# V is transposed in bulk beside the last two projection tiles; keys are transposed where V's chunk transposes stood

## The reference, cut to what matters

```python
h = rms_norm(x, p['g_pre']) * (1.0 + scale) + shift
z = h @ p['w_in']                       # 1024 -> 4096 columns
...
zc = centred_shift(zc, p['mu'])         # p + mu * (0.5 * (prev + next) - p)
r, k, v, lw, la = jnp.split(zc, [...], -1)
...
kk = kk * lax.rsqrt(jnp.sum(kk * kk, -1, keepdims=True) + 1e-12)
...
def step(s, inp):                       # per token, per head, s is value x key
    r_t, w_t, k_t, v_t, kk_t, a_t = inp
    sa = jnp.einsum('bhvk,bhk->bhv', s, kk_t)
    s = (s * w_t[:, :, None, :] - sa[..., None] * (kk_t * a_t)[:, :, None, :]
         + v_t[..., None] * k_t[:, :, None, :])
    return s, jnp.einsum('bhvk,bhk->bhv', s, r_t)
...
out = jnp.concatenate([ya, yb, yc], -1) @ p['w_out']
x = x + gate * rms_norm(out, p['g_post'])
```

## Time and profile before

| | us |
|---|---|
| median of 3 runs | 1085.96 (1084.84 to 1086.45) |
| the profiled execution | 1087.09 |
| its span, first to last instruction | 1085.3 |
| PE busy | 1005.1 (93%) |
| PEld busy | 907.3 (84%) |
| DVE busy | 641.6 (59%) |
| ACT busy | 426.4 (39%) |
| POOL busy | 409.3 (38%) |
| granted TensorE clock, mean | 0.972 of full |

### The profile page before, as it was taken

One profiled execution on the slowest core, in us unless ns is written; L12 is line 12 of the kernel. 1 busy time (PEld: TensorE's weight loads), 2 busy tenths in 40 slices (PEclk: granted clock), 3 DMA queues, 4 the chain that ended last, 5 costly groups with the idle time before them and its releaser, 6 DMA issues. The chain is left out here.

```text
span 1085.3 us, 31987 instructions
## 1 busy us (share of the span) xinstructions
PE 1005.1 (93%) x14375; PEld 907.3 (84%) x14375; DVE 641.6 (59%) x952; ACT 426.4 (39%) x708; POOL 409.3 (38%) x372
## 2 busy tenths in 40 slices
PE   5699999999999999994699999999999998899997
PEld 3399999999989888983699999999999997566685
DVE  5351059776457302245688888888888885546532
ACT  5361102100124332222355655666555665434311
POOL 8111112311205312322446555566676665512200
PEclk9699999999999999996699999999999999999999
DMA  9711422111122110000000000000000004421331
GB/s 356 268 37 62 178 84 79 40 39 39 39 83 81 42 39 1 1 1 11 1 4 4 4 4 4 4 4 5 4 4 4 4 4 159 135 109 35 121 117 59
DMA packets 30564, 61.46 MB, mean 57 GB/s; under 512 B 3368, under 2 KB 21972, under 8 KB 29276
## 3 DMA queue, kind: packets, MB, share of 16 engines
q1 hardware_dynamic: 30428, 59.42, 15.5%
HBM read 49.68 MB, written 9.73 MB: 55 GB/s over the span
## 5 line engine op out<-in xcount | busy, mean ns | idle before, releaser
L681 PE MATMUL ps<-input_rounded,weights_rounded 128*128 128x386 f32 x768 | 264.0, 344 | 4.1 <-DVE input_rest L788 2.8
L683 PE MATMUL ps<-input_rounded,weights_rest 128*128 128x386 f32 x768 | 260.7, 339 | 0.0
L682 PE MATMUL ps<-input_rest,weights_rounded 128*128 128x386 f32 x768 | 260.4, 339 | 0.0
L1464 POOL TENSOR_TENSOR arena<-arena,lvl 128x512 f32<-128x512 f32 x108 | 138.8, 1300 | 78.2 <-ACT arena L1372 46.4
L470 POOL TENSOR_TENSOR weights_rest<-arena,weights_rounded 128x2048 fp32r<-128x2048 f32 x16 | 75.8, 4737 | 211.2 <-ACT weights_rounded L515 211.2
L681 PEld LDWEIGHTS ps<-input_rounded,weights_rounded 128*128 128x128 f32 x768 | 145.1, 189 | 10.9 <-issue 7.5
L682 PEld LDWEIGHTS ps<-input_rest,weights_rounded 128*128 128x128 f32 x768 | 145.3, 189 | 0.5
L683 PEld LDWEIGHTS ps<-input_rounded,weights_rest 128*128 128x128 f32 x768 | 145.4, 189 | 0.0
L1157 PE MATMUL ps<-arena 64*64 64x64 f32 x2880 | 107.0, 225 | 18.1 <-issue 14.6
L1157 PEld LDWEIGHTS ps<-arena 64*64 64x64 f32 x2880 | 95.2, 138 | 23.8 <-issue 17.1
L1167 PE MATMUL ps<-arena 64*64 64x64 f32 x2880 | 104.9, 223 | 5.4 <-DVE arena L1595 4.1
(11 more groups left out here) (247 smaller groups left out, 1700.8 us busy)
## 6 DMA issues: line engine op xcount, KB each, us to landing
arena<-in_w_in SPq DMA_DIRECT2D x16, 1024.0 KB, 5.2
arena<-in_ada_w SPq DMA_DIRECT2D x7, 1024.0 KB, 5.3
mix_scratch<-zc SPq DMA_DIRECT2D x4, 1158.0 KB, 9.7
out<-arena SPq DMA_DIRECT2D x9, 512.0 KB, 2.6
zc<-in_x_sample SPq DMA_DIRECT2D x4, 1024.0 KB, 9.1
hT<-in_ada_w SPq DMA_DIRECT2D x4, 1024.0 KB, 12.1
zc<-in_w_out SPq DMA_DIRECT2D x4, 1024.0 KB, 8.6
arena<-in_x_sample SPq DMA_DIRECT2D x8, 512.0 KB, 3.7
```

The lines of the kernel that those rows point to most:

```text
L681: pe.matmul(o, w_hi[:, k, cut], hi_of_h[:, k, cols_b], start=(k == 0), stop=False)
L682: pe.matmul(o, w_hi[:, k, cut], lo_of_h[k][:, cols_b], start=False, stop=False)
L683: last = pe.matmul(o, w_lo[:, k, cut], hi_of_h[:, k, cols_b], start=False, stop=(k == KT - 1))
L1464: pool.tensor_tensor(Um[l % 3], UT, lvl[:, l, :].unsqueeze(1).to_broadcast([P, 2 * PAIRS, C]), ALU.mult).then_inc(q_um[l], 1)
```

## The change

V is no longer transposed chunk by chunk in the scan. Beside the last two tiles of the projection TensorE transposes the four V tiles in 36 blocks of 128 tokens (12 groups in banks 6 and 7), ScalarE alone copies them to two staging buffers in the weight ring, and SP stores them in a scratch tensor in DRAM (8 DMAs). In the scan SP loads each chunk's V by token (4 DMAs per chunk, 64 KB each, 72 in all) straight into its place. `transpose_v` and `v_by_token` leave the scan. `transpose_keys` moves from behind `gram(n1, 1)` to behind `product(n2, 4)`, from banks 4-5 to 6-7, and now waits for the second mask. The spreads of the key norm use banks 0 and 1 and wait for the tile before the last to be emptied; the reciprocal stands behind mix tile 9 instead of 11. The four roundings of `w_out` stand at other places.

```diff
 
+                def v_by_token(at):
+                    a, g = V_GROUPS[at]
+                    if a >= 2:
+                        act.wait_ge(s_vd[a % 2], 32)
+                    n = min(4, 9 - 4 * g) * P
+                    act.wait_ge(s_vp, at + 1)
+                    act.activation(v_stage[a % 2][:, 512 * g:512 * g + n], ps[:, 6 + at % 2, 0:n], ACT.Copy).then_inc(s_vs, 1)
...
 
+                def transpose_v(at):
+                    a, g = V_GROUPS[at]
+                    pe.wait_ge(s_mix, 9 + a)
+                    if at == 0:
+                        pe.wait_ge(s_kd, NB * PAIRS)
+                    if at >= 2:
+                        pe.wait_ge(s_vs, at - 1)
+                    for i in range(4 * g, min(4 * g + 4, 9)):
+                        c = TP if i == 0 else TS + P * (i - 1)
+                        last = pe.transpose(ps[:, 6 + at % 2, P * (i - 4 * g):P * (i - 4 * g) + P], vT[:, a, c:c + P], eye[:, :])
...
+                    if j >= V_AT:
+                        at = 2 * (NB * (j - V_AT) + b)
+                        transpose_v(at)
+                        transpose_v(at + 1)
...
                 pe.wait_ge(s_kr, 1)
+                pe.wait_ge(s_raw, MIXES - 1)
...
                         if at >= 2:
                             pe.wait_ge(s_kn, at - 1)
-                        pe.matmul(ps[:, 6 + at % 2, 0:NC], back[:, a, :], kn[:, n * NC:(n + 1) * NC],
+                        pe.matmul(ps[:, at % 2, 0:NC], back[:, a, :], kn[:, n * NC:(n + 1) * NC],
                                   start=True, stop=True).then_inc(s_kp, 1)
 
...
                                                  op0=ALU.mult, op1=ALU.add).then_inc(s_mix, 1)
-                        if i == 11:
+                        if i == 9:
                             dve.wait_ge(s_kd, NB * PAIRS)
                             dve.reciprocal(kn, kn).then_inc(s_kr, 1)
...
+                for a in range(4):
+                    block = v_stage[a % 2].rearrange("p (i c) -> p i c", i=9)
+                    sp.wait_ge(s_vs, NB * (a + 1))
+                    sp.dma_start(v_dram[TP:TP + SEQ, P * a:P * a + P], block[:, 0, :]).then_inc(s_vd[a % 2], 16)
+                    sp.dma_start(v_dram[TS:TS + DEC_SEQ, P * a:P * a + P].rearrange("(i p) c -> p i c", p=P),
+                                 block[:, 1:9, :]).then_inc(s_vd[a % 2], 16)
+                for h in range(2):
+                    sp.wait_ge(s_vd[h], 64)
                 sp.wait_ge(s_gst, 32)
                 sp.wait_ge(s_sg, 32)
...
+
+                def load_v(n):
+                    earlier(sp, q_state, n - 1)
+                    earlier(sp, q_yb, n - 1)
+                    for d in DIRS:
+                        rows = v_dram[STARTS[n][d]:STARTS[n][d] + C, :].rearrange("t (a g j) -> t g a j", a=PAIRS, g=2)
+                        for g in range(2):
+                            h = head(d, g, 0)
+                            sp.dma_start(UV[n % 2][OTHER[d], d, h:h + PAIRS, :], rows[:, g]).then_inc(q_vl[n % 2], 16)
+
+                sp.wait_ge(q_init, 1)
+                for n in range(N):
+                    load_v(n)
...
             @block.tensor
             def _(pe):
                 def lora(n):
-                    earlier(pe, q_kv, 2 * n)
+                    earlier(pe, q_m[0], 2 * n)
...
 
-                def transpose_v(n):
-                    earlier(pe, q_m[1], 2 * n)
-                    for d in DIRS:
-                        for a, g in HEADS:
-                            last = pe.matmul(ps[OTHER[d], 6 + (g ^ d), C * a:C * a + C], chunk(vT, n, d)[HALVES[g], a, :],
-                                             eyes[HALVES[g], :], start=True, stop=True)
-                    last.then_inc(q_vt, 1)
-
...
                     else:
-                        pe.wait_ge(q_v, 2 * (n + 1))
+                        earlier(pe, q_m[1], 2 * n)
+                        earlier(pe, q_kv, 2 * n)
                     for a, g in HEADS:
...
                 def transpose_keys(n):
-                    pe.wait_ge(q_m[0], 2 * (n + 1))
+                    pe.wait_ge(q_m[1], 2 * (n + 1))
                     for d in DIRS:
                         for a, g in HEADS:
                             at = C * (PAIRS * d + a)
-                            last = pe.transpose(ps[:, 4 + g, at:at + C], BK[HALVES[g], d, a, :, :].rearrange("p s c -> p (s c)"),
+                            last = pe.transpose(ps[:, 6 + g, at:at + C], BK[HALVES[g], d, a, :, :].rearrange("p s c -> p (s c)"),
                                                 eyes[HALVES[g], :])
                     last.then_inc(q_kt, 1)
 
...
                     earlier(pe, q_ye, 2 * n)
-                    pe.wait_ge(q_v, 2 * (n + 1))
+                    pe.wait_ge(q_vl[n % 2], 64 * (n // 2 + 1))
...
                         gram(n1, 1)
-                        transpose_keys(n1)
                     if n2 == N - 1:
                         final_state()
                     if 0 <= n2 < N:
                         product(n2, 4)
-                    if 0 <= n0 < N:
-                        transpose_v(n0)
+                    if 0 <= n1 < N:
+                        transpose_keys(n1)
                     if 0 <= n2 < N:
                         update(n2, 4)
...
 
-                def v_by_token(n):
-                    act.wait_ge(q_vt, n + 1)
-                    earlier(act, q_state, n - 1)
-                    earlier(act, q_yb, n - 1)
-                    for d in DIRS:
-                        act.activation(UV[n % 2][OTHER[d], d].rearrange("p (k a) c -> p k a c", k=2),
-                                       ps[OTHER[d], 6:8, 0:C * PAIRS].rearrange("p k (a c) -> p k a c", a=PAIRS),
-                                       ACT.Copy).then_inc(q_v, 1)
...
-                        act.activation(KBT[n % 2][:, :, PAIRS * g:PAIRS * g + PAIRS, :], by_channel(4 + g), ACT.Copy).then_inc(q_kv, 1)
+                        act.activation(KBT[n % 2][:, :, PAIRS * g:PAIRS * g + PAIRS, :], by_channel(6 + g), ACT.Copy).then_inc(q_kv, 1)
...
-                    if n2 == N - 1:
-                        round_w_out(0)
                     if 0 <= n3 < N:
                         copy_y(n3, 4)
+                    if n3 == N - 1:
+                        round_w_out(3)
                     if 0 <= n1 < N:
                         decay_tanh(n1)
                         decay_shift(n1)
...
                     if n2 == N - 1:
-                        round_w_out(1)
+                        round_w_out(0)
                     if 0 <= n1 < N:
                         decay(n1)
                         rate(n1)
...
                     if n2 == N - 1:
-                        round_w_out(2)
-                    if 0 <= n1 < N:
-                        v_by_token(n1)
+                        round_w_out(1)
                     if 0 <= n2 < N:
                         copy_y(n2, 3)
                     if n2 == N - 1:
-                        round_w_out(3)
+                        round_w_out(2)
                     if n2 == N - 1:
                         act.wait_ge(q_fs, 1)
                         act.activation(S[0], by_channel(5), ACT.Copy).then_inc(q_fc, 1)
```

More of the change, by code:

```diff
@@ L68 @@
 MIXES = TILES.count("mix")
+V_GROUPS = [(a, g) for a in range(4) for g in range(3)]
 RING = 3
@@ L130, in hybrid_step_kernel @@
         gate_dram = nc.dram_tensor("gate_scratch", [2, D_MODEL], F32, kind="Internal").ap()
+        v_dram = nc.dram_tensor("v_scratch", [W, PAIRS * P], F32, kind="Internal").ap()
         mix_dram = nc.dram_tensor("mix_scratch", [8, P, W], F32, kind="Internal").ap()
@@ L227, in hybrid_step_kernel @@
         ss, rs = small[:, 0:9], small[:, 9:18]
+        v_stage = [ring[:, slot_of("z", len(PIECES) - 3 + h), 0:9 * P] for h in range(2)]
+        V_AT = len(TILES) - 2
         part1 = ExitStack()
@@ L283, in hybrid_step_kernel @@
         s_lwt = sem1("lw_tanh_ready")
+        s_vp = sem1("v_transposed")
+        s_vs = sem1("v_by_token")
+        s_vd = [sem1(f"v_stored_{h}") for h in range(2)]
         s_cv = sem1("conv_b_done")
@@ L552, in layer_norm @@
                         act.activation(T[:, 2 + g, :], T[:, g, :], ACT.Tanh, scale=0.5).then_inc(s_lt, 1)
+                def v_by_token(at):
[5 more added lines that the diff above has]
+                    act.activation(v_stage[a % 2][:, 512 * g:512 * g + n], ps[:, 6 + at % 2, 0:n], ACT.Copy).then_inc(s_vs, 1)
                 round_weights(1)
                 for j, kind in enumerate(TILES):
+                    if j >= V_AT:
+                        for at in range(2 * NB):
+                            v_by_token(2 * NB * (j - V_AT) + at)
                     h, z = j % 2, zbanks(j)
@@ L663, in kk_norm @@
                                   start=True, stop=True).then_inc(s_ks, 1)
+                def transpose_v(at):
[8 more added lines that the diff above has]
```

(9 more changed lines are left out.)

## The result

The changed kernel takes 1108.77 us (median of 4 runs, 1107.49 to 1110.14); the kernel before took 1086.11 beside it (4 runs). The ratio is 1.0211 [1.0199, 1.0223]: slower by 22.7 us, where 1109 had been predicted. The profiled execution took 1109.95 us (span 1108.1), 22.8 more than that of before.

What follows compares the result with a forecast made beforehand. Each scan step was taken as bound by a loop through several engines, not TensorE's busy share; 18.6 + 0.2 - 0.5 + 4.9 = +23.2 us gave 1109 us, own range 1102 to 1116, 8 in 10 range 1096 to 1119.

Steps and rivals of the forecast that it cites:

- Scan: In the scan's 16 periods, the later keys delay triangle, mask, inverse and biases, lengthening periods to about 23.47 us: +18.6 us.
- slack: In an early scan step, the chain keys, triangle, mask, inverse has 0.64 us to spare against the chain over TensorE.
- 1.00 us of place: In an early scan step, time from the second mask's end to the biases grows by 1.64 - 0.64 = 1.00 us.
- the early steps' sum: VectorE's decay sum in early scan steps grows from 1.50 to 2.2 us as in late ones, adding 0.3 us of period.
- V in bulk: In the projection, V's 36 transposes at 0.136 us each add whole to TensorE: +4.9 us, bounds 0 and 10.
- Start: At the scan's start, 1.39 us gained from V's products of chunk 0, about 1.6 lost in the next step: +0.2 us.
- End: At the scan's end, moving the first w_out rounding gains 1.4 us, the late inverse loses 0.9: -0.5 us.
- TensorE's queue is the bound: Rival: removing V's 0.89 us from TensorE counts in each of 18 chunks, 16.0 us, giving 1074.9 us; chance 0.09.
- Half hidden: Rival: ScalarE or GpSimd make up part of the scan's delay, 0.5 us a step remain: +12.6, 1098.5 us; chance 0.10.
- the clock falls in the scan: Rival: more TensorE idle time lowers the granted clock, a step lasts about 10 us longer; three give 1139; chance 0.05.
- V loads late: Rival: V's loads or stores come late for the scan; at 1 us a step 1125 us; chance 0.03.
- the two cancel: Rival: the queue's gain and the chain's loss in the scan cancel within 0.2%; chance 0.03.

Runs made afterwards that it cites:

- the doses of 16 and 24 copies: Kernel before with ScalarE's two keys' copies cut into 16 or 24 smaller ones, so the triangle starts later: 1089.86 us and 1098.65 us.
- the run with V in bulk alone: Projection of the changed kernel (V transposed and stored in bulk) with the scan of the kernel before, so V is transposed twice: 1092.11 us, ratio 1.0048.
- the run with the keys' move undone: Changed kernel with the keys' transposes back ahead of the level-4 product in banks 4 and 5, V still out of the scan: 1088.61 us, ratio 1.0022.
- the order alone: Kernel before with triangle gathered first on ScalarE, GpSimd's level-5 mask ahead of the bonus keys, its level-2 mask held back: 1085.25 us, ratio 0.9997.

## Why the prediction was right, and where it was off

**Scan, predicted +18.6, measured +18.9.** The mechanism and each link are as predicted: the keys' transposes 0.05 us behind the mask (0.06), the triangle 1.64 us later (1.70), a slack of 0.64 (0.73, by the doses of 16 and 24 copies), 1.00 us of place (0.97), and the early steps' sum as long as the late ones' (0.3 predicted; 0.34 by the run with 16 copies). Period forecast 23.45 to 23.48, measured 23.47. It was right because the slack was read on the one engine where both chains meet, as VectorE's 0.64 us of idle ahead of the biases, and not from busy shares. The slack is a little more than the idle time, because in the kernel before the inverse of an early step did not wait for the level-0 mask. The mask had ended at 704.11; the inverse began at 704.20 behind VectorE's transpose of level 4:

```profile
703.56 0.72 DVE L1599 STREAM_TRANSPOSE arena<-ps 128x512 f32<-128x512 f32 x1 [0.59 <-PE ps L1167]
```

Where it does wait, it begins 0.03 behind the mask and the biases 0.61 behind it (719.22, 719.25, 719.86 in the changed kernel). From 704.11 that makes 704.75, which is 0.74 ahead of 705.49.

**V in bulk, predicted +4.9, measured +4.4.** The mis-sized term is the transposes' spacing: 0.136 us in the row taken, 0.110 between these, 36 of them 3.96 us. (The 0.096 and the 3.9 us in some of the expectations come from the 3.44 us with the drift still in it.) From the end of VectorE's last mix (L922, now L966) to the scan's first instruction it took 1.54 us in place of 1.12, 0.4 more. The stores of V are not what it waits for: the last is issued at 488.57 and they take 3.0 us median, so they had landed some 7 us before the mix ended at 498.84. What the 0.4 is stays open; the run with V in bulk alone has it too. The loads take 2.4 us median, and no wait of the scan is put down to them, as predicted.

**Start, predicted +0.2, measured +0.18.** First biases 1.38 us earlier against the scan's start (1.39), 1.56 us lost up to the first level-4 product of a full step (1.6). Only 1.24 of it stands between the first two biases (21.15 us in place of 19.91). The rest comes behind them, where the lower clock reached closer to that product: it ended some 2.4 us ahead of it before (0.73 in 540 to 545, product at 545.11) and 0.9 after (0.67 in 545 to 550, product at 549.16). So the close match of the 1.6 may be in part luck.

**End, predicted -0.5.** The level-5 update of that step came at 932.18 against 909.28, +22.90, where the level-4 product stood at +22.96: -0.06. The rounding moved away as planned, but the update then waited 0.69 us for VectorE's factor. What came instead was not foreseen. Before, the granted clock was at its lower level for some 3.4 us from about 928 on (0.84 in 925 to 930, 0.82 in 930 to 935), where TensorE had just idled for 0.86 us (after, the same idle time comes without a fall). Two windows, and one product of that stretch:

```profile
925.00:930.00 5.00, 3.35 (x82) 3.11 (x80) 2.07 (x4) 2.70 (x3) 5.00 (x2) 0.84 0.19 30
...
929.00:930.00 1.00, 1.00 (x24) 1.00 (x22) 0.00 (x0) 0.00 (x0) 1.00 (x1) 0.50 0.42 66
```

```profile
928.17 1.82 PE L1157 MATMUL ps<-arena 64*64 64x64 f32 x32 [0.86 <-issue]
```

The same product of the changed kernel, at 1.00:

```profile
951.34 1.15 PE L1206 MATMUL ps<-arena 64*64 64x64 f32 x32 [0.86 <-issue]
```

It starts 23.17 us later than before; the next product behind the stretch (934.00 before, 955.67 after) only 21.67 later. After, the clock stays at 1.00 up to the end of the scan and falls in 960 to 965 (0.66), behind the 1.89 us in which TensorE waits at the barrier. The first product after the scan is thus only 21.7 us later, 1.2 won back, and the rest of the kernel is 1.1 longer. In sum: scan +18.9, V in bulk +4.4, start +0.2, end -0.1, clock -1.2 and +1.1, and -0.5 since the profiled execution after was 0.52 us ahead when V's transposes began: +22.8, the difference of the spans. Each term lies within about 0.5 us of its forecast; the drift had none. That the median hits 1109 within 0.3 us is luck, since the four runs spread over 2.7 us.

**The rivals.** *TensorE's queue is the bound* falls for this change: with V's work gone and nothing late, the step was as long as before. The Trainium skill, "Perfetto Trace Analysis", section "Identifying the Most-Contended Engine", would have had the engine with the 92% of weight loads made lighter; the run with the keys' move undone made it lighter by 0.89 us a step and gained none of it, so this trace does not bear the rule out. But the rival had a true core that I priced at nothing: the *order* of TensorE's queue sets the other chain of the same meeting point, and together with the earlier triangle it was worth a whole microsecond of place (4.07 to 3.08). By the two lines above, with the triangle's end left at 1.35, an estimate gives up to 0.73 of it to TensorE's order alone; that was not run. *Half hidden*, *the clock falls in the scan* (1.00 from 560 to 900 us), *V loads late* and *the two cancel* did not happen.

## What to carry to other kernels

Where two chains meet on an engine that runs in order, look for its idle time directly ahead of the meeting: that is the slack of the one chain and the handle on the other. Shortening the chain that is not the last gives nothing (the order alone, 1085.25 us), and shortening the last one can give no more than the distance to the next; here the two lay 0.73 us apart. The gain came when both were shortened, the later one by moving half of its work into a gap in which TensorE waited anyhow, and then a third chain was the last. Moving a step later moves all that is queued behind its consumers: the keys' copies were needed by no one soon, the triangle behind them was. And give a dose in small steps and read what it really was before judging the theory by it.

## What the runs showed of the hardware

- Small ScalarE copies out of PSUM, issued one behind the other, cost 0.065 us more per piece: 1024 columns in 2, 3, 4, 6, 16 and 24 pieces took 1.08, 1.15, 1.21, 1.34, 1.97 and 2.48 us in all. One of 32 columns in the row of 24 is recorded with 0.27 us on average, since they overlap.
- VectorE's decay sum of 528 columns takes 1.26 us where no GpSimd mask runs beside it. In the early step of before a mask ran beside it for 0.39 us and it took 1.50; in the changed kernel for 1.79 us, and it took 2.24: more than half of each overlapped us is added. A GpSimd mask that started beside it took 1.73 us instead of 1.27. Ending the overlap by one wait on GpSimd went with 3.6 us off the kernel (1076.98 to 1073.34).
- 36 transposes of 128x128 in fp32, in six batches of 8 or 5 between the column blocks of the last two projection tiles, added 3.96 us to TensorE's queue, 0.110 each, where eight in a row at the start of the kernel are shown as 1.09 us.
